# An RWKV block, a short-conv block and an attention/FFN block on one core: GLU units from unnormalised rows, ScalarE clamps in attention, gates in even steps, idle TensorE filled with small matmuls

## The reference

```
x = x + short_conv_mix(rms_norm(x, b_norm))          # end of the first part
x = rms_norm(x, final_norm)
h = rmsnorm(x, norm_mix_pre)                         # third block
conv_in, q, k, v, g_conv, g_att = split(h @ w_in)    # 1024, 512, 512, 512, 1024, 1024 columns
u = glu(conv_in);  u = 31-tap causal depthwise conv(u) + bias
u = silu(layernorm(u));  conv_out = u @ w_conv_branch + b
# attention, 8 heads of 64, strictly causal, z = q k / 8:
log_1m = log_sigmoid(-z) (0 where masked);  rev = reverse exclusive cumsum(log_1m)
a = exp(log_sigmoid(z) + rev);  att = a @ v
merged = sigmoid(g_conv) * conv_out + sigmoid(g_att) * (att @ w_att_branch)
x = x + rmsnorm(merged @ w_out, norm_mix_post)
h = rmsnorm(x, norm_ffn_pre);  x = x + rmsnorm((silu(h @ Wg) * (h @ Wu)) @ Wd, norm_ffn_post)
```

## Time and profile before

| | |
|---|---|
| median of 3 runs (range) | 2197.27 us (2197.24 to 2198.46) |
| the profiled execution | 2199.01 us |
| its span, first to last instruction | 2197.3 us |
| TensorE matmuls busy | 2049.6 us, 93% |
| VectorE busy | 1416.5 us, 64% |
| ScalarE busy | 995.4 us, 45% |
| mean granted TensorE clock | 0.977 |

### The profile page before, as it was taken

How to read it: one execution, slowest core, us unless ns; L and a number is a source line. 1 busy time by engine, 2 the same in 40 slices (tenths; PEclk the granted TensorE clock), 3 DMA queues, 4 the chain that set the end, 5 groups by cost and what they waited for, 6 DMA issues and landing times.

```text
span 2197.3 us, 43117 instructions
## 1 busy us (share of the span) xinstructions
PE 2049.6 (93%) x16706; PEld 1632.8 (74%) x16706; DVE 1416.5 (64%) x2261; ACT 995.4 (45%) x1751; POOL 169.5 (8%) x183
## 2 busy tenths in 40 slices
PE   5999999978888887999999999999899989999997
PEld 4877777767777775888888888778566867887875
DVE  7778888866666664355654555688885655445355
ACT  6656666636665655232222223332666234333243
POOL 5120000012322223000000000000000000000000
PEclk9999999989999998999999999999999989999998
DMA  4445555633333311333233333233112312333332
GB/s 119 120 137 172 175 175 172 177 93 81 86 85 92 71 33 68 96 87 104 86 101 91 96 95 94 78 93 99 37 40 76 97 57 86 99 92 91 95 87 81
DMA packets 395950, 215.16 MB, mean 98 GB/s; under 512 B 85137, under 2 KB 374313, under 8 KB 395817
## 3 DMA queue, kind: packets, MB, share of 16 engines
q1 hardware_dynamic: 395608, 213.18, 33.6%
q10 hardware_dynamic: 208, 0.06, 0.0%
HBM read 181.68 MB, written 31.52 MB: 97 GB/s over the span
## 4 chain that ended last, share of the span: by engine, by line
PE 82%; DVE 9%; ACT 5%; issue 3%; SPq 1%; DMA 1%; ACTq 0%; DVEq 0%
PE bank L1680 23%; PE bank L1681 22%; PE bank L1682 22%; PE bank L565 3%; PE bank L542 1%; PE bank L573 1%; PE bank L474 1%; PE bank L488 1%; PE bank L516 1%; DVE w_lo L1927 1%; PE bank L495 1%; ACT inv L717 1%; PE bank L554 1%; PE bank L1800 1%; PE bank L508 1%
## 5 line engine op out<-in xcount | busy, mean ns | idle before, releaser
L1680 PE MATMUL bank<-xl,w_hi 128*128 128x512 f32 x1680 | 673.1, 401 | 22.2 <-DVE w_lo L1927 8.3
L1681 PE MATMUL bank<-xl,w_lo 128*128 128x512 f32 x1680 | 660.8, 393 | 0.0
L1682 PE MATMUL bank<-xl,w_hi 128*128 128x512 f32 x1680 | 659.1, 392 | 0.0
L1357 ACT ACTIVATE w_hi<-w_raw 128x1024 fp32r<-128x1024 f32 x280 | 294.2, 1051 | 358.5 <-PE bank L1682 357.8
L1927 DVE TENSOR_TENSOR w_lo<-w_raw,w_hi 128x1024 fp32r<-128x1024 f32 x280 | 343.3, 1226 | 118.7 <-ACT w_hi L1357 112.5
L1680 PEld LDWEIGHTS bank<-xl,w_hi 128*128 128x128 f32 x1680 | 317.4, 189 | 122.2 <-issue 42.0
L1682 PEld LDWEIGHTS bank<-xl,w_hi 128*128 128x128 f32 x1680 | 317.1, 189 | 71.4
L1681 PEld LDWEIGHTS bank<-xl,w_lo 128*128 128x128 f32 x1680 | 317.7, 189 | 66.8 <-issue 2.2
L1680 PE MATMUL bank<-xh,w_hi 128*128 128x512 f32 x480 | 198.1, 413 | 15.7 <-DVE xh L1932 13.9
L1681 PE MATMUL bank<-xh,w_lo 128*128 128x512 f32 x480 | 189.8, 395 | 0.0
L1682 PE MATMUL bank<-xh,w_hi 128*128 128x512 f32 x480 | 189.5, 395 | 0.0
(11 more groups left out here) (357 smaller groups left out, 2922.5 us busy)
## 6 DMA issues: line engine op xcount, KB each, us to landing
w_raw<-in_a_w_in SPq DMA_DIRECT2D x64, 512.0 KB, 4.2
w_raw<-in_b_w_in SPq DMA_DIRECT2D x64, 512.0 KB, 4.1
w_raw<-in_w_ffn_up SPq DMA_DIRECT2D x44, 512.0 KB, 4.0
...
```

The costliest lines, as they stand in the source:

```text
L1357: A(w_hi[0:rows, slot, 0:nkb, 0:ncol], w_raw[0:rows, slot, 0:nkb, 0:ncol], ACT.Copy).then_inc(s_hi, 1)
L1680: mm(outp, wh, xlo, start=start, stop=False)
L1681: mm(outp, wl, xhi, start=False, stop=False)
L1682: return mm(outp, wh, xhi, start=False, stop=stop)
```

## The change

1. **GLU from unnormalised rows.** The last 8 conv output units also make `xl[2]` = rows times both gains, split (ScalarE `hi`, VectorE `low`). The first four GLU units multiply that (`phase(U_GLU, 2, 2, xl[2], X_U, then=lambda: norm(2))`), and VectorE multiplies by the reciprocal root when it empties their banks (`glu_value`, `glu_gate`). The tiles of `xh` are made among this; `norm(3)` stands behind the fourth unit.
2. `final_norm` moves from the GLU pairs into the output units of the third block; its root has a place of its own, `r_final`.
3. **Taps**: 12 and 13 in the last two GLU pairs (9 and 10 before), 6 in each QKV unit (5 and 6), 5 ahead of attention (3), and 4, 1, 0, 0 in the four steps of a group (2 each), the rest behind attention.
4. **Attention**: ScalarE makes the clamps of the 512-wide items (as Relu). Gates are served in even steps: ScalarE's weight copy at the step's start, VectorE's part between L1006 and L1012, ScalarE's sigmoid at the step's end. ScalarE alternates between the two items: Exp, Ln, `att_a`, Exp, Ln, `att_a`.
5. **Layer norm**: first halves of two tiles each in steps 3 and 4, second halves in steps 4 to 6 (one, two, one); the sigmoids get buffers of their own (`silu`).
6. **Spins**: 8 and 18 matmuls of 128x128 into an unused bank ahead of and behind `norm(4)`, 7 and 12 around `norm(6)`.
7. **FFN start**: the square of a tile comes one tile later on ScalarE, and the third unit's weights are prepared ahead of the root.

```diff
-TAPS_GLU = [(0, 0, 0), (2, 2, 0), (3, 4, 2), (4, 4, 2)]
+TAPS_GLU = [(0, 0, 0), (0, 0, 0), (4, 5, 3), (5, 5, 3)]
+TAPS_STEP = [4, 1, 0, 0]
...
+        LN_FIRST = {3: (0, 1), 4: (2, 3)}
+        LN_LAST = {4: (0,), 5: (1, 2), 6: (3,)}
...
-            return GATES_FIRST + step // 2 if step % 2 else None
+            if step == STEPS + 1:
+                return GATES_LATE
+            return GATES_FIRST + step // 2 - 1 if step and step % 2 == 0 else None
+
+        def clamped_by_scalar(m):
+            return item(m)[1] == 0
...
+                        A(att_sp[:, item(m)[0] % 2, item(m)[4]], logits(m), ACT.Relu).then_inc(s_pos, 1)
+                if gate is not None:
+                    gate_weights(gate)
...
+                if half:
+                    even(base + 4 * KB, DK // 2, xT2, 2, hi=xl[2], gain=lambda k: both_gains[:, k:k + 1])
...
             ahead(U_GLU, 2, 0, 0)
+            ahead(U_GLU, 2, 0, 1)
             norm(2)
-            for k in range(DK):
-                x_high(X_H3 + k, xh[:, 0, k, :], k % 2)
+            glu_high(0, 1)
+            ahead(U_GLU, 2, 1, 0)
...
-            norm(2)
-            norm(3)
...
+            def spin(count):
+
+                for n in range(count):
+                    c = n % 4
+                    mm(bank[6][:, c * P:(c + 1) * P], ident[:], mean_d[:], start=True, stop=True)
...
-            two_units(U_GLU, xh, X_H3)
-            phase(U_GLU, 2, CT + 3 * AT // 2, xh, X_H3, started=True)
+            phase(U_GLU, 2, 2, xl[2], X_U, then=lambda: norm(2))
+            norm(3)
+            phase(U_GLU + 4, 2, CT - 2 + 3 * AT // 2, xh, X_H3)
...
+            spin(8)
             norm(4)
+            spin(18)
...
+            def glu_value(j):
+                dve.wait_ge(s_unit, U_GLU + 2 * j + 1)
+                V.tensor_tensor(glu[:, j, PAD2:], bank[0][:], r_glu, ALU.mult).then_inc(s_free[0], 1)
```

More of the change, by code:

```diff
@@ L298, in program @@
         cen = [over(f"cen{j}", [P, T]) for j in range(CT)]
+        spot += 2048
+        silu = [over(f"silu{j}", [P, T]) for j in range(CT)]
+        assert spot <= last_at
         spot = x_at
@@ L985, in attention_scalar @@
                         A(att_a[:, h % 2, cols], logits(m), ACT.Exp).then_inc(s_wt, 1)
-                gate(gate_at(step))
+                if gate is not None:
+                    gate_sigmoid(gate - 1)
                 if when(step - 2, STEPS) and (step - 2) % NT == NT - 1:
@@ L1017, in attention_vector @@
                         ins.then_inc(s_sp, 1)
-                    for _ in range(2):
+                    for _ in range(TAPS_STEP[step % NT]):
                         next(tap, None)
-                gate(gate_at(step))
+                else:
+                    gate(gate_at(step))
                 if step == STEPS + 1:
@@ L1617, in layer_norm @@
                     A(z, z, ACT.Exp, scale=-1.0).then_inc(s_ls, 1)
+                for j in LN_LAST.get(step, ()):
                     x_high(X_UC + j, uc[:, 0, j, :], j % 2)
@@ L2095, in _, with even @@
                                 ALU.subtract).then_inc(s_xlo, 1)
-            def even(base, turns, dst, add, n=None, final=False, low=None, gain=None, x0=None):
+            def even(base, turns, dst, add, n=None, final=False, low=None, gain=None, x0=None, each=None):
                 if n is not None:
@@ L2124, in turn @@
                             V.tensor_tensor(acc[:], acc[:], sq[:, u, :], ALU.add).then_inc(s_sqa, 1)
+                        if each is not None:
+                            each(2 * t + u)
                 repeat(dve, turns - final, turn)
@@ L2230, in _ @@
                 more(TAPS_GLU[j][1])
-                dve.wait_ge(s_unit, n0 + 2)
-                V.tensor_scalar(rstd[:, j % 2, :], bank[1][:], CLAMP, None, ALU.max).then_inc(s_free[1], 1)
-                for k in range(4 * j, 4 * j + 4 if j < 2 else 0):
-                    final_norm(k)
+                glu_gate(j)
                 more(TAPS_GLU[j][2])
-                dve.wait_ge(s_glu, j + 1)
-                V.tensor_tensor(glu[:, j, PAD2:], rstd[:, j % 2, :], glu[:, j, PAD2:], ALU.mult).then_inc(s_gluok, 1)
-                dve.wait_ge(s_gluok, j + 1)
+                glu_product(j)
             for n in range(3 * AT):
                 w_low(U_QKV + n + 1, (n + 1) % 2)
-                more(5 + n % 2)
+                more(6)
             def gate2(n):
@@ L2277, in layer_norm @@
                             V.tensor_tensor(acc[:], acc[:], sq[:, j % 2, :], ALU.add).then_inc(s_lacc, 1)
-                if step >= 3:
-                    j = step - 3
+                for j in LN_FIRST.get(step, ()):
                     y = cen[j][:]
@@ L2285, in layer_norm @@
                     V.tensor_scalar(y, y, col("conv_ln_b_2", j), CLAMP, ALU.add, ALU.max).then_inc(s_lz, 1)
+                for j in LN_LAST.get(step, ()):
                     dve.wait_ge(s_ls, j + 1)
-                    finish(j, lambda where: V.tensor_tensor(where, y, sq[:, j % 2, :], ALU.mult))
+                    finish(j, lambda where: V.tensor_tensor(where, cen[j][:], silu[j][:], ALU.mult))
             gate2(0)
-            more(3)
+            more(5)
             attention_vector(dve, o, split(X_AT, ah, AT), gate2, tap, lambda: layer_norm(0))
@@ L2340, in ffn @@
                     n0 = 2 * t + base
-                    if not first:
-                        w_low(n0 + 1, 1)
+                    w_low(n0 + 2 if first else n0 + 1, 0 if first else 1)
                     dve.wait_ge(s_unit, n0 + 1)
```

170 lines of the change are left out of this document (123 added, 47 removed).

## The result

| | before | after |
|---|---|---|
| median (range) | 2197.26 us (2196.87 to 2198.46, 4 runs) | 2171.2 us (2169.68 to 2177.75, 4 runs) |
| profiled execution, its span | 2199.01, 2197.3 us | 2170.37, 2168.7 us |
| TensorE matmuls busy | 2049.6 us | 2037.3 us |
| VectorE, ScalarE busy | 1416.5, 995.4 us | 1416.9, 1002.9 us |
| mean granted TensorE clock | 0.977 | 0.986 |

The ratio is 0.9882, with a 95% interval of 0.9866 to 0.9898: 26.1 us faster, where 17.4 were forecast.

A forecast was written before the change was run, and what follows sets the result against it. TensorE was taken as the bound, at 5.49 us a unit. The terms 8.2 + 2.0 + 3.6 + 3.2 + 0.4 = 17.4 us took the median from 2197.27 to 2179.9 us; forecast 2176.5 to 2183, range 2171.5 to 2188.5.

The forecast's parts named there:

- GLU start: From the last conv unit through GLU: 10.2 us won by unnormalised rows, 2.0 given back, net 8.2 us.
- the two late `w_lo`: Last GLU pairs: VectorE's extra taps make the next weights late, so TensorE stands still 0.45 and 1.55 us.
- Attention: Attention steps: 3.7 us of TensorE's waits for att_a won, 1.7 lost to a clock drop, net 2.0 us.
- The first step: Attention's first step has 4 taps in place of 2; its wait grows from 1.37 to 2.9 us.
- 1.8 us of further waits: Attention after its first wait: four of 0.15 us at 512-wide blocks, three of 0.4 us at scores behind them.
- Rival (a): Attention locks step, second block's exponentials held behind att_a: 2204 us; decides from 1.1 us a step; chance 0.05.
- Gates behind attention: Last gate units up to the second merge unit: two tiles' sigmoids per step, 3.6 us won; 1.8 with a clock drop.
- FFN start: FFN start: spins hold the clock, later square and earlier weights; fourth unit starts 3.2 us earlier despite a 1.2 us wait.
- the forecast's own sign: FFN start: if the clock falls with the spins in place, that step is wrong; expected clock 1.00 from 1765 to 1800.
- End: Last transposes of the kernel: end 0.4 us earlier if 19 spins keep the clock; ends 0 and 0.8.
- Rival (d): No late queue in GLU and no clock drops: 2.0 + 1.7 + 2.4 us more won, 2174 us; chance 0.18.
- rival (b): Spins don't hold the clock or overrun their pauses: 2.5 to 4 us less won, 2183 to 2188 us; chance 0.20.

The follow-up runs named there:

- the kernel with the old distance: The changed kernel with neg_ka and the two gain tiles placed behind the weights, so weights sink 64 bytes and rows stay: 2186.12 us, ratio 0.992.
- the repeat: The changed kernel, untouched, measured and profiled again: 2173.6 us, ratio 0.987 to the kernel before.
- the distances of 128 and 32: The kernel before with row_sum and row_rstd behind hT and a gap of 128 or 32 bytes ahead of xx: 2216.69 and 2220.93 us.
- the control run of the kernel before: The kernel before, unchanged, profiled once more: 2200.91 us in one run.

## Why the forecast was near in most steps and wrong in its sum

**The step that failed** is the forecast's first conclusion: "Everything that the diff touches lies behind 1365 us, so the 1365 us ahead stay", and with it the unit of 5.49 us in every later term. It read the diff for instructions, and took the two lines that move `row_sum` and `row_rstd` for bookkeeping. They change the distance of weights and rows, and so the time of 6,720 matmuls: 9.2 us in the kernel before, 11 to 12.5 in the changed one. Without it, by the kernel with the old distance, the sum came out at 15.5 to 17.6 us, by how it is measured, for 17.4 forecast. That they agree so well is partly luck; by steps:

1. **GLU start**, forecast 8.2. At the old distance 8.0. The conv units stayed unbroken, the chain through the unnormalised rows was in time, and the two late `w_lo` cost 0.72 and 1.46 us for 0.45 and 1.55. Right, for the reason given.
2. **Attention**, forecast 2.0. At the old distance 4.9, after the change 4.8, and nothing by the placement alone: the term was too small. The first step was right, 2.67 us for 2.9, and so was the drop of the clock behind it. But of 1.8 us of further waits (4 x 0.15 and 3 x 0.4) none came, since the value was taken from the time of ScalarE's three ACTIVATEs and not from a chain followed through both engines. The waits fell by 5.7 us and not by 3.7. Rival (a), that attention's steps lock because an `att_a` stands ahead of the second block, is out: none locked, and undoing the order cost 6.0 us. The Trainium skill ("TensorE: Matmul & The Clock Gate", section "Architectural detail: the array is 16× 32×32, not 1× 128×128") says that ScalarE's queue is in strict order, by which such a wait holds all that is behind it. The trace agrees: ScalarE waited for TensorE's sums ahead of 13 of the 32 `att_a`, 13.1 us together (3 and 4.0 before), and in four steps the second block's exponentials stood behind such a wait, of 0.25 or, three times, 0.80 us, as here:

```profile
1554.85 0.28 ACT L1012 ACTIVATE att_a<-bank 128x128 f32<-128x128 f32 x1 [0.80 <-PE bank L954]
```

That is under the 1.1 us a step from which the rival decides, and TensorE had other work in the meantime: after the first step it waited for no `att_a`.

3. **Gates behind attention**, forecast 3.6. After the change 4.5, of which 0.8 is the pace (132.0 us in the kernel before with only the placement, for 132.8): 3.7. The waits were 2.02 and 0.46 for 2.4 and 0.6. At the old distance it was 2.0, with the drop behind the pause for which the forecast named 1.8. Right.
4. **FFN start**, forecast 3.2, measured 1.7 from the mean to the fourth unit: 36.9 us before (1785.51 to 1816.92 and one unit), 35.2 after. Too large, and by the forecast's own sign, the clock falling with the spins in place, wrong. The wait at the fourth unit came, 1.11 for 1.2, and the first unit came 6.72 us behind the mean where 7.65 were before. The two units that follow took longer than I had counted: a pause of 0.90 us in them, 0.86 more at the third unit, and a drop of 3.4 us behind the second pause, in spite of the spins. In the repeat without that drop 3.1 us were won. The 3.4 us in the table for the whole stretch are half this and half the pace; there two errors hid each other.
5. **End**, forecast 0.4, measured 0 in this pair of traces. The clock fell again between the last transposes. Over all traces, though, it is 17.4 to 18.2 us with spins (seven) and 18.1 to 19.1 without (ten), so the term was about right.

The two sizes that were off, +2.9 in attention and -1.5 in the FFN, nearly cancel. Rival (d), no late queue and no drops, gave 2174, nearest to the result; it didn't happen, since both late `w_lo` and the drop in attention are in the trace, so by the time alone the wrong story would have been believed. And the 2188 at rival (b)'s upper end isn't the sum of its terms, which give 2185.7.

How much of the 7.1 us ahead of E is pace? One pair of traces can't tell, since the clock was low for 58.0 us ahead of 1400 before and for 44.4 after. All 17 traces tell more: E lies at 1409.4, 1412.0 and 1413.0 us in the three at the old distance, at 1402.1 to 1409.7 in the twelve at a quick one (mean 1405.7), and at 1423.0 and 1423.9 at the distances of 128 and 32. So near 6 us are pace. The clock was low for 41 to 75 us there, and costs less than half of that time: the control run of the kernel before had 13.7 us more of it and ended 2.6 us later.
